# RMS norms of a two-layer encoder trunk: which operand of the sum-of-squares matmuls stays in the array

## What is computed

```python
def rms_norm(x, g):
    y = x32 * lax.rsqrt(jnp.mean(x32 * x32, axis=-1, keepdims=True) + EPS)
    return (y * g.astype(jnp.float32)).astype(x.dtype)
...
for i in range(DEPTH):
    mod = cond @ mod_w[i] + mod_b[i]
    sh1, sc1, g1, sh2, sc2, g2 = jnp.split(mod, 6, axis=-1)
    h = modulate(rms_norm(x, norm_mix_g[i]), sh1, sc1)
    y = dsa_attention(...) if i == 0 else s5_layer(...)
    x = x + g1[:, None, :] * y
    h = modulate(rms_norm(x, norm_ffn_g[i]), sh2, sc2)
    x = x + g2[:, None, :] * conv_ffn(h, ...)
return rms_norm(x, final_g)
```

## Time and profile before

| | |
|---|---|
| runs | 769.78, 769.33 and 773.53 us, median 769.78 |
| profiled execution | 771.09 us, of which the span from first to last instruction is 769.3 |
| PE busy | 723.5 us (94%) |
| PEld busy | 656.4 us (85%) |
| DVE / ACT / POOL busy | 539.0 (70%) / 407.4 (53%) / 129.8 (17%) us |
| matmuls of the squares, L465 | 80 records for 40 matmuls |
| turning matmuls, L472 | 20 records for 10 matmuls |
| mean granted TensorE clock | 0.991 |

### The profile page before, as it was taken

The page is one execution under the profiler, slowest core; times in us unless marked ns, Lnnn a source line. Parts: engine busy times, 40 slices in busy tenths (PEclk is TensorE's granted clock), DMA queues, the critical chain, the costliest instruction groups (busy, mean ns, idle before and its releaser), DMA issues.

```text
span 769.3 us, 17309 instructions
## 1 busy us (share of the span) xinstructions
PE 723.5 (94%) x6636; PEld 656.4 (85%) x6636; DVE 539.0 (70%) x959; ACT 407.4 (53%) x674; POOL 129.8 (17%) x121
## 2 busy tenths in 40 slices
PE   4789999989999999999998899988999999999995
PEld 1478999458798999999997789978969999999994
DVE  5766656985578878787876866675567767676665
ACT  4354645555465656657557542334556555555553
POOL 1000000211014333333440544540000000000000
PEclk9899999999999999999999999999999999999998
DMA  8989654896756676757573221029526555555521
GB/s 320 377 301 405 224 186 137 327 390 255 278 183 200 256 241 216 260 190 272 188 273 116 79 77 64 2 80 375 196 67 196 184 176 178 190 190 166 189 82 55
DMA packets 46068, 156.61 MB, mean 204 GB/s; under 512 B 6016, under 2 KB 7312, under 8 KB 46016
## 3 DMA queue, kind: packets, MB, share of 16 engines
q1 hardware_dynamic: 43344, 148.26, 55.0%
q10 hardware_dynamic: 2160, 6.38, 2.1%
q0 software_dynamic: 512, 1.25, 0.5%
HBM read 154.82 MB, written 1.05 MB: 203 GB/s over the span
## 4 chain that ended last, share of the span: by engine, by line
PE 80%; DVE 8%; ACT 4%; DMA 4%; issue 2%; SPq 1%; POOL 1%; DVEq 0%; ACTq 0%; POOLq 0%
PE up L364 14%; PE up L366 14%; PE up L365 14%; PE acc L364 8%; PE acc L365 8%; PE acc L366 8%; PE gv L406 4%; DMA raw<-in_w 1%; DMA ffn<-in_mw 1%; DVE tmp L1172 1%; DVE hl L1177 1%; DVE wlo L1141 1%; ACT whi L813 1%; PE acc L733 1%; DMA ident<-in_ident 1%
## 5 line engine op out<-in xcount | busy, mean ns | idle before, releaser
L1141 DVE TENSOR_TENSOR wlo<-raw,whi 128x1024 fp32r<-128x1024 f32 x188 | 252.2, 1356 | 99.1 <-ACT whi L813 94.3
L364 PE MATMUL up<-hh,whi 128*128 128x256 f32 x896 | 255.8, 285 | 2.0 <-DVE hl L1177 1.9
L365 PE MATMUL up<-hl,whi 128*128 128x256 f32 x896 | 253.5, 283 | 0.0
L366 PE MATMUL up<-hh,wlo 128*128 128x256 f32 x896 | 253.5, 283 | 0.0
L813 ACT ACTIVATE whi<-raw 128x1024 fp32r<-128x1024 f32 x185 | 192.4, 1051 | 42.9 <-PE acc L366 20.4
L364 PEld LDWEIGHTS up<-hh,whi 128*128 128x128 f32 x896 | 171.8, 192 | 10.1 <-issue 4.1
L365 PEld LDWEIGHTS up<-hl,whi 128*128 128x128 f32 x896 | 171.9, 192 | 0.0
L366 PEld LDWEIGHTS up<-hh,wlo 128*128 128x128 f32 x896 | 171.9, 192 | 0.0
L1475 DVE SCALAR_TENSOR_TENSOR ffn<-up,conv,ffn 128x254 f32<-128x254 f32 (+1 forms) x176 | 72.7, 475 | 44.3 <-ACT ffn L1006 43.9
L364 PE MATMUL acc<-ah,whi 128*128 128x256 f32 x352 | 99.7, 283 | 0.1
L365 PE MATMUL acc<-al,whi 128*128 128x256 f32 x352 | 99.6, 283 | 0.0
(11 more groups left out here) (233 smaller groups left out, 916.3 us busy)
## 6 DMA issues: line engine op xcount, KB each, us to landing
raw<-in_w SPq DMA_DIRECT2D x188, 512.0 KB, 3.6
mraw<-in_mw SPq DMA_DIRECT2D x48, 512.0 KB, 6.2
arena<-in_mw SPq DMA_DIRECT2D x24, 512.0 KB, 10.2
raw<-in_w SPq DMA_DIRECT2D x12, 256.0 KB, 12.9
tmp<-in_mw SPq DMA_DIRECT2D x6, 512.0 KB, 7.6
ffn<-in_mw SPq DMA_DIRECT2D x6, 512.0 KB, 8.7
tmp<-in_mw ACTq DMA_DIRECT2D x4, 512.0 KB, 6.9
ffn<-in_mw ACTq DMA_DIRECT2D x4, 512.0 KB, 9.7
```

The source lines that it names most:

```text
L364: pe.matmul(out, w_h, xh, start=first, stop=False, skip_group_check=skip)
L365: pe.matmul(out, w_h, xl, start=False, stop=False, skip_group_check=skip)
L366: return pe.matmul(out, w_l, xh, start=False, stop=last, skip_group_check=skip)
L1141: dve.tensor_tensor(wlo[:, n % SPL, :], raw[:, n % RAW, :], whi[:, n % SPL, :].bitcast(F32), ALU.subtract).then_inc(lo_ready, 1)
```

## The change

In the eight steps of a norm the operands swap roles: for each tile k, the squares of 128 tokens are stationary and a column of ones moves, once for each half of the tokens, and all sixteen matmuls add into columns 8 and 9 of misc. The start flag is on the first of the sixteen alone. The copy of the rows and the turning matmuls are gone, with their semaphores, and so is the memset of misc. ACT's root waits for the last of the sixteen.

```diff
@@ norm(), on PE
                     pe.wait_ge(sq_ready, KT * n + k + 1)
-                    mm = pe.matmul(misc[32 * (k % 4):32 * (k % 4) + 1, T:2 * T], ones[:, 0:1], tmp[:, k, :],
-                                   start=(k < 4), stop=(k >= 4))
-                mm.then_inc(ssum, 1)
+                    for h in range(2):
+                        mm = pe.matmul(misc[:, 8 + h:9 + h], tmp[:, k, h * P:(h + 1) * P], ones[:, 0:1],
+                                       start=(k == 0 and h == 0), stop=(k == KT - 1), skip_group_check=True)
+                mm.then_inc(csum, 1)
                 if first:
                     first()
-                pe.wait_ge(sum_row, n + 1)
-                for h in range(2):
-                    mm = pe.matmul(misc[:, 8 + h:9 + h], gm[:, h * P:(h + 1) * P], picks[:, 0:1], start=True, stop=True)
-                mm.then_inc(csum, 1)
                 if meanwhile:
                     meanwhile()
@@ PE, at the start and before norm 3
-            pe.wait_ge(set_up, 5)
+            pe.wait_ge(set_up, 4)
...
-            pe.wait_ge(set_up, 6)
+            pe.wait_ge(set_up, 5)
@@ root(), on ACT
             def root(norm):
-                act.wait_ge(ssum, norm + 1)
-                if norm:
-                    act.wait_ge(cols_done, (0, C_OUT // 2, C_SIN // 2, C_GLU // 2, CH)[norm])
-                act.activation(gm[:, 0:T], misc[:, T:2 * T], ACT.Copy).then_inc(sum_row, 1)
                 act.wait_ge(csum, norm + 1)
                 act.activation(rt[:], misc[:, 8:10], ACT.Sqrt, scale=1.0 / D, bias=epsc[:, 0:1]).then_inc(rt_ready, 1)
@@ DVE, at the start
-            dve.memset(misc[:], 0.0).then_inc(set_up, 1)
```

More of the change, by code:

```diff
@@ L214, in build @@
         m_early = [sem(f"m_early{j}") for j in range(3 * MS)]
-        sum_row, csum = sem("sum_row"), sem("csum")
+        csum = sem("csum")
         x_in = sem("x_in")
@@ L233, in build @@
         x_upd = sem("x_upd")
-        sq_ready, ssum, rt_ready, ri_norm, hp_ready = (
-            sem("sq_ready"), sem("ssum"), sem("rt_ready"), sem("ri_norm"), sem("hp_ready"))
+        sq_ready, rt_ready, ri_norm, hp_ready = (
+            sem("sq_ready"), sem("rt_ready"), sem("ri_norm"), sem("hp_ready"))
         act_hi, act_lo = sem("act_hi"), sem("act_lo")
```

## The result

The changed kernel takes 783.54 us (median of 6 runs, 781.75 to 787.65) against 773.52 us (median of 6, 769.33 to 774.22) for the one before: ratio 1.0161, 95% interval 1.0139 to 1.0183. It is slower, as forecast, but by 12.4 us of 773.5 and not by 6.9, and 783.5 lies above the stated range of 772.3 to 779.5. Two later jobs, each on a chip of its own, gave 1.0166 (1.0138 to 1.0193) and 1.0134 (1.0099 to 1.0168).

What follows compares the result with a forecast made beforehand. The prediction took PE's records one behind the other to bound the kernel. Norms 0 to 4 gave 2.9 + 1.8 + 0 + 1.8 + 0.4 = 6.9 us, on 769.8 us 776.7 us; range 772.3 to 779.5.

Steps and rivals of the forecast that it cites:

- what one record costs: PE's sums in the norms: a full fp32 load takes 0.111 us a record at 2.4 GHz, 0.20 us at 1.2 GHz.
- the sum: All five norms together: 6.9 us slower.
- norm 1's spread: Norm 1: longer sums delay filler, root and spread, +1.8 us; norm 3 the same.
- norm 2's spread: Norm 2: the sums end earlier, but DVE's weight splits hold the reciprocal, so 0, a gain of 0.1 us at best.
- norm 4's first output tile: Norm 4: 32 records outlast the saved copy and turning, +0.4 us, and only the output follows.
- norm 0: Start of the kernel: 32 loads at 1.2 GHz make gemv(0) begin at 16.3 instead of 13.43, +2.9 us.
- the third case: All norms: loads hidden at 0.04 us a record, removed steps pure gain, -4.4 us, 765.4 us; chance 0.06.
- my fourth case: Norms 1 to 4: the clock falls during the thin matmuls, 791 us; chance 0.08.
- The likeliest case: All norms as worked out, norms 1 to 4 at 2.4 GHz: 776.7 us; chance 0.50.
- the second case: Norm 0: the clock rises by the end of the sums, cost there 0.7 us, 774.5 us in all; chance 0.22.
- the fifth case: After norm 0: a wait further on takes up its delay, leaving 4.0 us, 773.8 us; chance 0.14.
- its cover: Norm 2: DVE's two weight splits, 2.36 us, hide PE's sums, which may take 1.0 us longer before they cost anything.

Runs made afterwards that it cites:

- e1: The changed kernel with 64 columns of ones moving instead of one: 778.88 us against 771.40 for the kernel before, ratio 1.0092.
- e7: The changed kernel with 64 columns of ones moving, repeated beside the changed kernel on one chip: 778.94 us, ratio 1.0086 to the kernel before.
- e4: The kernel before with the new form in norms 2 and 4 alone: 770.74 us against 771.40, ratio 0.9999.
- e11: The changed kernel with 64 columns moving in norms 1 and 3 alone, one column elsewhere: 780.73 us against 771.40 for the kernel before, ratio 1.0115.
- e6: The changed kernel run once more, unaltered: 785.98 us against 772.23 for the kernel before, ratio 1.0166.
- e10: The kernel before with the new form in norms 1 to 4, norm 0 in the old form: 780.88 us against 771.40, ratio 1.0107.
- norm 0 alone: The kernel before with the new form in norm 0 only, norms 1 to 4 in the old form: 773.68 us against 771.40, ratio 1.0022.
- the parts: The kernel before with the new form in norms 1 and 3 alone, 775.79 us, and in norms 2 and 4 alone, 770.74 us, both against 771.40.

## Why the prediction was wrong

**What held: the loads.** The step "what one record costs" was right. It took 0.111 us from the two-column rows and the loads came at 3.21 us for 28, against 3.19. With the clock out of the way (e1, e7) the whole change costs 7.1 us (4.8 to 9.3) and 6.6 us (5.0 to 8.2), and the sum said 6.9; that it fits to a few tenths is partly luck, since its terms are each off a little. Its terms against the profile of e1, each counted from the first load of the norm: norm 1's spread 2.07 us later than before, 6.88 against 4.81, forecast 1.8; norm 3 the same by its root; norm 2's spread 0.3 us earlier, 5.31 against 5.61, forecast 0; norm 4's first output tile 5.42 against 4.98, forecast 0.4, came 0.4; norm 0 in the changed kernel 3.2 instead of 2.9. The gap of 25 ns for small matmuls in the Trainium skill (page "TensorE: Matmul & The Clock Gate", section "Back-to-back issue gap"), by which the third case would have come about, isn't the pace of a record that brings its own full fp32 load: 0.111 us here.

**What failed: the clock, my fourth case.** The likeliest case took 2.4 GHz for norms 1 to 4. I gave the fall of the clock a chance of 0.08 and argued against it that "here weights are loaded throughout". That is the step that failed. Weights were loaded throughout, PE and PEld read busy 5.00 of 5.00, and the clock fell all the same, during the last thin matmuls or right behind them, in norms 1, 2 and 3. The fall that I had compared it with was of another kind: in the kernel before it came behind a stretch in which PE had almost nothing to do:

```profile
22.00:24.00 2.00, 0.17 (x2) 0.08 (x1) 1.59 (x5) 0.61 (x2) 0.00 (x0) 1.00 1.03 407
24.00:26.00 2.00, 0.76 (x4) 0.59 (x5) 1.43 (x4) 0.51 (x1) 0.00 (x0) 0.90 1.04 414
26.00:30.00 4.00, 3.11 (x13) 2.07 (x17) 2.84 (x7) 2.86 (x6) 0.00 (x0) 0.50 1.03 410
```

That fall was no sign that a PE which loads weights throughout keeps the clock: a busy PE with one moving column lost it too. In the same text I had written, against the second case, that "a matmul that moves one column keeps the array all but idle". The Trainium skill's page "TensorE: Matmul & The Clock Gate", Part 1, puts the level down to how busy PE has been; by the profile's busy time that would have kept it up here, and the runs decide that it is not this time that counts. I used my own sentence for norm 0, where it meant that the clock wouldn't rise, and not for norms 1 to 4, where it means that it may fall. One reading of the array's activity belonged to both.

The size of the fourth case was wrong too: 14 us on top, where the changed kernel has 5.3 over e1 (ratios 1.0161 and 1.0092, from two jobs) and 7.0 over e7 in one job. It priced all 28 thin records at the low pace, 2.5 us in each of norms 1 and 3. They ran at the full pace in norm 1, 3.21 us for 28 in all five profiles with one column there, and in norm 3 in three of five (3.21 or 3.22; 3.93 and 4.04 in the others); the low level comes mostly behind them. In norm 2 the 32 loads took 3.65 us (forecast 3.63) in three of six such profiles, and 3.93, 4.57 and 4.99 in the others. What pays is the filler (3.16 instead of 1.90 us) and what stands behind it. In norm 4, priced at 3.3, it was little: the root came 3.79 us after the first load in four of six profiles with one column there (4.49 and 4.96 in e4 and e11; 3.84 with 64 columns in e1 and e7), and the spread took 1.22 us instead of 0.71 in five of the six.

**The range.** It held the fifth case and the second, but left out the fourth, and its upper end came from the pace and gemv(1) alone. The 64-column kernel, whose clock stayed up in norms 1 to 3, lies inside it in both jobs, at 778.9. The base was off as well: the forecast stands on 769.8, the median of three runs, and six gave 773.5, so 3.7 of the 6.8 us between 776.7 and 783.5 are the base. With the new base the range would be 776.0 to 783.2, and 783.5 still lies above it.

**Smaller steps.** Norm 0: I wrote that the table load in front of ACT's root would lie beside PE's work. It doesn't; it waits for the sums like the root, from 16.81 to 18.09. It cost nothing, for gemv(0) took 3.59 us in the meantime. The second case, a rise during the sums, didn't happen: gemv(0) took 3.59 us as before. The fifth, norm 0 taken up later: up to norm 1 it isn't; over the whole, norm 0 alone costs 1.7 us of its 3.2, so a part of it may be; the interval, 0.2 to 3.2 us, holds both ends. Norm 2: its cover held against the loads at their full pace, and the spread's matmuls behind it took 1.2 us in place of 0.7 at the low level. Where the clock fell during the loads it didn't hold: the spread came 6.5 and 6.9 us after the first load in e6 and e10, against 5.6 before.

**Still open.** Why the parts (5.0 and 0) don't make e10's 8.3, what decides whether the low level lasts 3 or 14 us in norm 3, and what in the array's work counts for the clock: the runs tell one moving column from 64, and no more.

## What to carry to other kernels

Making the wide tensor stationary to get its sums out as a column trades a moving pass for a full weight load; in fp32 that was 32 records at 0.111 us against 16 (fourteen of them loaded at under 0.04 us each) and 4 full ones, and it saved a 0.38 us copy. Count the records behind one another on PE first. Then ask what the array itself does in them: a PE that reads busy with one-column matmuls did not keep the clock up here, and the bill came in the work behind. If such a form is wanted anyway, letting 64 columns move instead of one cost no time at this pace (3.22 us for 28 records) and kept the clock up.

## What the runs showed that was not expected

The granted clock fell to 0.50 in or right behind the matmuls that move one column in all 16 such norms, and in the changed kernel's norms 1 and 3 PE and PEld were busy all the time ahead of it; with 64 columns behind the same loads it stayed at 1.00 in all eight such norms of three profiles (norms 1 to 3 of e1 and e7, 1 and 3 of e11). A DVE reciprocal of 128x256 fp32 took 1.75 us, where 128x2 took 0.17. An fp32 matmul record with a full stationary operand and 256 columns took 0.22 us, though the fp32r one takes 0.12, and fourteen fp32 loads of one stationary column each, whose results are spread over four groups of rows of the output, came at under 0.04 us each. Low stretches at the start have other lengths from profile to profile of one and the same kernel, 7 or 14 us in the kernel before, so a part of any difference between two single profiles can be chance.
